# Two layers of a hybrid diffusion backbone on one core: the opening's loads and turns in another order, turned tiles repeated at the seams, and weight splits, gate blocks and one pair of loads moved

## The chip, the cores and the metric

The kernel runs on one core of a Trainium2 chip, as one launch, with nothing else on the chip. The time is the device time of one launch in microseconds. The engines of the core are named as in the profile: PE is TensorE (matmul; PEld its weight load), DVE is VectorE, ACT is ScalarE, POOL is GpSimd and SP is SyncE, which here issues all DMAs. Every engine runs its own instruction list in order and waits on semaphores that other engines raise.

## What is computed

The reference is one inference step of `DEPTH = 2` layers over 128 prompt tokens and 256 sample tokens of width 1024, all in float32. The two groups share the weights.

```python
def layer(x, mod, p, latent, ckv_ctx, krope_ctx, hf0, hb0):
    sh1, sc1, g1, sh2, sc2, g2 = jnp.split(mod, N_MOD, axis=-1)
    h = rms_norm(x, p["g_pre_mix"]) * (1.0 + sc1) + sh1
    y, ckv, krope, hf, hb = mixer(h, p, latent, ckv_ctx, krope_ctx, hf0, hb0)
    x = x + g1 * rms_norm(y, p["g_post_mix"])
    h = rms_norm(x, p["g_pre_ffn"]) * (1.0 + sc2) + sh2
    x = x + g2 * rms_norm(swiglu(h, p), p["g_post_ffn"])
    return x, ckv, krope, hf, hb
```

`mod` is `silu(c) @ w_mod + b_mod`, with six parts per layer. The mixer multiplies `h` by one wide `w_in` and takes from it the queries' and keys' latents, the input and gate of a bidirectional recurrence (a convolution over four tokens, sigmoid gates from block-diagonal weights, two scans over the tokens), and two merge gates. Attention of 8 heads and the recurrence are projected (`w_o_mla`, `w_o_lru`), merged by the gates and projected again (`w_out`). The feed-forward part is a SwiGLU with 2816 hidden channels.

## The kernel before

**Products.** Activations lie with channels on the partitions, in chunks of 128 channels by 384 tokens. Each weight block is a *job* of a few loads of 128x1024 elements. To keep float32 accuracy each operand is split in a high and a low part, and each product is three matmuls: high by high (line 669), high by low (676) and low by high (677). A job's eight chunks take four output banks each. ACT makes the high part of a load (`highs`, line 1180), DVE the low part (`lows`, line 1556). Both walk the same list of loads, and a call names how far the walk is to have come, so that moving a call moves a 128x1024 instruction to another place of that engine's list. There are 3 buffers for raw loads, 5 for each part, and 2 for weights of `w_mod`. SP waits for a raw buffer to be free (line 553) or for a `w_mod` buffer (line 560), and nothing behind the waiting issue goes out.

**Order.** The order of work on each engine is written out by hand. `plan_loads` sets the order of the loads. On TensorE the jobs run one after the other: `lx0`, `lx1` (the recurrence's input), `qk`, `kr` (latents), `gg0`, `gg1` (its gate), four merge jobs, the up-projections, `ol0` and `ol1` with attention woven in, `om0`, `om1`, `wo`, eleven `fi` jobs and `fo`. `gates_between` puts a gate block of the recurrence (four banks, lines 896 to 898) behind a given product of a job: a product is one of the 32 pairs of 676 and 677. Some jobs *host* products of the next modulation with `w_mod` in spare columns of their banks (`HOSTED`, line 708), after their first and third load.

**Recurrence on DVE and ACT.** Per chunk, ACT applies the gates and exponentials (`lru_gates`, `lru_coefficients`); DVE does `squared_roots`, `scans` (two directions, line 1804 to 1818), `gated` and `xc_low`, between the low parts of the weights.

**Seams.** Where a norm lies between two jobs (from `wo` to `fi0` in both layers, from `fo` to the next layer's `lx0`), the result stands with tokens on the partitions, in tiles 1, 2 (samples) and 0 (prompt), taken in that order. For each tile and half, ACT sums squares of the result (`y_square`), DVE scales it and adds it to `x` (`residual`), ACT sums squares of the new `x` and forms the inverse root (`x_square`: square, `sum_bias`, square, `root`), and writes it as a diagonal matrix `rstd`. TensorE multiplies `x` by the diagonal (line 629), which turns it to channels on the partitions and scales it at once (`turned`, `turn_first`). Then DVE and ACT make the activation's high and low part, chunk by chunk (`normalise`, `act_highs`).

**Opening.** SP loads the conditioning rows (`cache_c`), `ident`, `fold`, `x`, then 2 MB blocks of `w_mod` (`first_mod`) in two halves (`FIRST`), with the small parameter rows between. TensorE first transposes the conditioning rows, from which ACT makes `cs`; it turns the three tiles of `x`, multiplies the blocks by `cs` (`first_product`, line 838) and folds the sums (`first_fold`, line 848). The second half's products and folds stand inside job `lx0` (`opening_between`). The chunks 4 to 7 of `x` reuse the banks of the chunks 0 to 3, once ACT has moved those.

## Time and profile before

| what | value |
|---|---|
| median of 3 runs | 1329.72 us (1329.58 to 1330.15) |
| profiled execution | 1329.25 us, span 1327.5 us |
| TensorE busy | 1283.3 us, 97% of the span |
| DVE busy | 813.7 us, 61% |
| ACT busy | 661.8 us, 50% |
| granted TensorE clock, mean | 0.994 of full speed |
| DMA | 147 GB/s from HBM over the span |

The profiled execution is one launch of its own. Its span runs from the first to the last recorded instruction, and its time is what the launch reported. Busy time of TensorE is modelled: matmuls overlap, so an engine at 97% may still lose time at a lower clock. Granted clock 1.00 is 2.4 GHz and 0.50 is 1.2 GHz.

### The profile page before, as it was taken

Reading aid. Unit: us, or ns where it says so; the run is one execution under the profiler, and the core shown is the slowest. Engines: PE = TensorE matmul, PEld = TensorE weight load, DVE = VectorE, ACT = ScalarE, POOL = GpSimd, SP = SyncE. Lnnn points to the kernel's source line nnn. Section 1 sums busy time; section 2 is a strip of 40 time slices with the busy share of each in tenths; the row PEclk is TensorE's granted clock in tenths of the full one; section 3 lists DMA queues with packets and bytes.
Section 4 is the critical chain, followed back from the end, with each engine's and each line's share of the span. In section 5 each row is a group of like instructions: output and inputs, shape, how many; then the busy total and the mean of one; then the engine's idle time right before and its main releaser. Section 6 shows DMA issues by size and latency. Waiting matters only on the chain.

```text
span 1327.5 us, 20006 instructions
## 1 busy us (share of the span) xinstructions
PE 1283.3 (97%) x7691; PEld 1177.8 (89%) x7691; DVE 813.7 (61%) x1410; ACT 661.8 (50%) x1173; POOL 18.3 (1%) x38
## 2 busy tenths in 40 slices
PE   6999999999999999999999989999999999999998
PEld 4898999977879999998789989998788899999886
DVE  2687584763759877743367785747566785444424
ACT  4478873753454323342264989537444533333422
POOL 0000000200000000000000000002000000000000
PEclk9999999999999999999989999999999999999999
DMA  9535555323427766534325444553225374444431
GB/s 336 190 113 163 186 156 190 103 95 115 139 75 217 222 207 207 155 129 156 105 64 158 129 162 161 158 197 125 89 72 159 98 234 134 127 127 127 159 108 67
DMA packets 135058, 196.21 MB, mean 148 GB/s; under 512 B 9730, under 2 KB 68268, under 8 KB 134964
## 3 DMA queue, kind: packets, MB, share of 16 engines
q1 hardware_dynamic: 134964, 194.94, 45.9%
q8 instruction: 61, 1.00, 0.3%
q14 instruction: 33, 0.27, 0.1%
HBM read 193.03 MB, written 1.88 MB: 147 GB/s over the span
## 4 chain that ended last, share of the span: by engine, by line
PE 84%; DVE 5%; ACT 5%; DMA 3%; issue 2%; SPq 1%; DVEq 0%; ACTq 0%
PE bank L669 17%; PE bank L676 17%; PE bank L677 17%; PE bank L764 6%; PE bank L763 6%; PE bank L762 6%; DVE weight_low L1556 2%; PE bank L708 2%; DMA first_mod<-in_w_mod 2%; ACT weight_high L1180 1%; PE bank L1054 1%; PE bank L629 1%; PE bank L744 1%; PE bank L1078 1%; ACT sq L1188 1%
## 5 line engine op out<-in xcount | busy, mean ns | idle before, releaser
L676 PE MATMUL bank<-act_low,weight_high 128*128 128x384 f32 x1440 | 487.2, 338 | 4.6 <-DVE weight_low L1556 2.4
L677 PE MATMUL bank<-act_high,weight_low 128*128 128x384 f32 x1440 | 482.5, 335 | 0.0
L1556 DVE TENSOR_TENSOR weight_low<-raw,weight_high 128x1024 fp32r<-128x1024 f32 (+5 forms) x282 | 319.5, 1152 | 177.2 <-ACT weight_high L1180 176.7
L1180 ACT ACTIVATE weight_high<-raw 128x1024 fp32r<-128x1024 f32 (+5 forms) x282 | 273.4, 995 | 246.5 <-PE bank L764 77.1
L669 PE MATMUL bank<-act_high,weight_high 128*128 128x384 f32 x1440 | 316.5, 340 | 1.8 <-DVE t L1660 1.8
L676 PEld LDWEIGHTS bank<-act_low,weight_high 128*128 128x128 f32 x1440 | 271.2, 188 | 11.6 <-issue 4.9
L677 PEld LDWEIGHTS bank<-act_high,weight_low 128*128 128x128 f32 x1440 | 271.1, 188 | 0.0
L669 PEld LDWEIGHTS bank<-act_high,weight_high 128*128 128x128 f32 x1440 | 253.1, 189 | 8.4 <-issue 4.5
L762 PE MATMUL bank<-weight_high,hid_high 128*128 128x512 f32 x264 | 104.4, 395 | 0.0
L764 PE MATMUL bank<-weight_high,hid_low 128*128 128x512 f32 x264 | 102.8, 389 | 0.0
L763 PE MATMUL bank<-weight_low,hid_high 128*128 128x512 f32 x264 | 102.8, 389 | 0.0
L1518 ACT ACTIVATE sq<-bank 128x384 f32<-128x384 f32 x44 | 19.3, 490 | 149.7 <-PE bank L677 149.7
L2086 DVE TENSOR_TENSOR t<-bank,sq 128x384 f32<-128x384 f32 x44 | 24.5, 558 | 93.2 <-PE bank L677 90.0
L763 PEld LDWEIGHTS bank<-weight_low,hid_high 128*128 128x128 f32 x264 | 49.6, 188 | 11.2 <-issue 1.0
L762 PEld LDWEIGHTS bank<-weight_high,hid_high 128*128 128x128 f32 x264 | 49.6, 188 | 11.1 <-issue 1.0
L764 PEld LDWEIGHTS bank<-weight_high,hid_low 128*128 128x128 f32 x264 | 49.6, 188 | 10.3
L1472 ACT ACTIVATE sq<-bank 128x384 f32<-128x384 f32 (+1 forms) x48 | 20.2, 420 | 54.6 <-PE bank L1078 27.5
L629 PE MATMUL bank<-rstd,x 128*128 128x128 f32 x192 | 32.5, 321 | 15.1 <-ACT rstd L1226 13.3
L629 PEld LDWEIGHTS bank<-rstd,x 128*128 128x128 f32 x192 | 29.3, 226 | 20.1 <-issue 16.1
L2025 DVE TENSOR_REDUCE negmax<-bank 128x1 f32<-128x384 f32 (+1 forms) x48 | 22.1, 465 | 31.8 <-PE bank L1054 31.7
L762 PE MATMUL bank<-weight_high,act_high 128*128 128x512 f32 x96 | 39.0, 407 | 0.0
L1579 DVE SCALAR_TENSOR_TENSOR qkv<-mod_weight,cs,qkv 128x512 f32<-128x512 f32 x56 | 38.5, 746 | 0.0
(238 smaller groups left out, 1553.2 us busy)
## 6 DMA issues: line engine op xcount, KB each, us to landing
raw<-in_w_ffn_in SPq DMA_DIRECT2D x176, 256.0 KB, 3.7
mod_weight<-in_w_mod SPq DMA_DIRECT2D x80, 512.0 KB, 4.7
raw<-in_w_in SPq DMA_DIRECT2D x72, 512.0 KB, 4.5
raw<-in_w_ffn_out SPq DMA_DIRECT2D x44, 512.0 KB, 3.7
first_mod<-in_w_mod SPq DMA_DIRECT2D x4, 2048.0 KB, 15.1
raw<-in_w_o_lru SPq DMA_DIRECT2D x16, 512.0 KB, 3.7
raw<-in_w_out SPq DMA_DIRECT2D x16, 512.0 KB, 3.7
raw<-in_w_o_mla SPq DMA_DIRECT2D x8, 512.0 KB, 6.0
```

The costliest lines, as they stand in the source:

```text
L629: ins = nc.tensor.matmul(turn_bank(job, c)[:, P * a:P * a + P], x[:, a, P * c:P * c + P], rstd[:, P * a:P * a + P], start=True, stop=True)
L669: nc.tensor.matmul(bank(job, g)[:, 0:T], view[0][:, kk, cols], high[:, k, :], start=k == 0, stop=False)
L676: nc.tensor.matmul(o, view[0][:, kk, cols], low[:, k, :], start=False, stop=False)
L677: ins = nc.tensor.matmul(o, view[1][:, kk, cols], high[:, k, :], start=False, stop=k == total - 1)
L708: ins = nc.tensor.matmul(bank(job, b)[32 * q:32 * q + 32, T:512], cs[:, k, :], modw[MIDX[n] % MODR][:, 512 * kk + P * b:512 * kk + P * b + P],
L762: nc.tensor.matmul(o, high[:, k, toks], view[0][:, kk, :], start=k == 0, stop=False)
L763: nc.tensor.matmul(o, high[:, k, toks], view[1][:, kk, :], start=False, stop=False)
L764: ins = nc.tensor.matmul(o, low[:, k, toks], view[0][:, kk, :], start=False, stop=k == 2 * pairs - 1)
L1180: nc.scalar.activation(high, w, ACT.Copy).then_inc(*AC.step())
L1556: nc.vector.tensor_tensor(low, w, high.bitcast(F), ALU.subtract).then_inc(*VE.step())
L1579: nc.vector.scalar_tensor_tensor(out=total(r, g), in0=w, scalar=c, in1=total(r, g), op0=ALU.mult, op1=ALU.add).then_inc(*VE.step())
L2086: nc.vector.tensor_tensor(t[c % 2][:, :], bank(f"fi{j}", 2 + g)[:, 0:T], sq[c % 4][:, :], ALU.mult).then_inc(*VE.step("hid", c))
```

## The change

Eight edits are made together.

- SP issues `x_prompt`, `ident` and `x_sample` first, then the conditioning rows and `fold`.
- TensorE runs the first half's first product before it turns tile 2, and turns the chunks 4 to 7 together ahead of the second product. In `normalise` of layer 0, DVE makes the low part of a weight one chunk later.
- The third and fourth quarter of the `w_mod` block that `ol1` hosts are loaded behind `om0`'s first load instead of ahead of it.
- The four gate blocks of `qk` stand behind products 5, 11, 17 and 23 instead of 9, 13, 20 and 25.
- In `turn_first`, TensorE repeats the turns of the chunks 2 and 3 of the tiles 1 and 2 (four matmuls with the same operands into the same banks), ahead of the wait for tile 0.
- At a seam, ACT leaves out `sum_bias` of tile 0's new `x`. DVE computes the same number behind `residual`, once ACT's first square is done, and ACT waits for it before `root`.
- ACT makes the high parts of `gates1`'s first load and of `gg1`'s first load together, earlier; and those of `gg1`'s third load and `gates1`'s second load together, one gate earlier.
- DVE makes the low part of `gg0`'s third load ahead of `scans(0, 0)`, those of `gg1`'s first and `gates1`'s first load ahead of `scans(2, 2)`, `gg1`'s second ahead of `scans(3, 3)`, and `gates1`'s second ahead of `gated(5)`.

```diff
--- before.py
+++ after.py
@@ -100,8 +100,10 @@
                 loads.append(Load(("sum", r), 2, 512, False, [("rows", "w_mod", 2 * q, 2, r * 512, 512, 0)]))
-            if job in HOSTED and i in (0, 3):
+            if job in HOSTED and (i == 0 or i == 3 and job != "ol1"):
                 mod(HOSTED[job], (0, 1) if i < 3 else (2, 3))
+            if (job, i) == ("om0", 0):
+                mod(HOSTED["ol1"], (2, 3))
             if i in (0, 2) and gates_after is not None:
@@ -433,12 +435,12 @@
         def _(sp):
+            sp.dma_start(x[:, 0, :], A["x_prompt"].rearrange("b t d -> (b t) d")).then_inc(start_x[0], 16)
+            sp.dma_start(ident[:, :], A["ident"]).then_inc(start_load, 16)
+            sp.dma_start(x[:, 1:3, :], A["x_sample"].rearrange("b (a p) d -> p (b a) d", p=P)).then_inc(start_x[1], 16)
             sp.dma_start(cache_c[0:C, 0:P], A["c_ctx"].rearrange("(n p) -> n p", p=P)).then_inc(start_load, 16)
             sp.dma_start(cache_c[C:2 * C, 0:P], A["c"].rearrange("b (n p) -> (b n) p", p=P)).then_inc(start_load, 16)
-            sp.dma_start(ident[:, :], A["ident"]).then_inc(start_load, 16)
             sp.dma_start(fold[:, :], A["fold"]).then_inc(start_fold, 16)
-            sp.dma_start(x[:, 0, :], A["x_prompt"].rearrange("b t d -> (b t) d")).then_inc(start_x[0], 16)
-            sp.dma_start(x[:, 1:3, :], A["x_sample"].rearrange("b (a p) d -> p (b a) d", p=P)).then_inc(start_x[1], 16)
 
@@ -806,6 +808,10 @@
                             turned(atp, pre, job, c, (a,), f"turn{a}", layer=lp)
+                    for a in (1, 2):
+                        for c in (2, 3):
+                            nc.tensor.matmul(turn_bank(job, c)[:, P * a:P * a + P], x[:, a, P * c:P * c + P], rstd[:, P * a:P * a + P],
+                                             start=True, stop=True)
                     for c in range(4):
@@ -861,21 +867,19 @@
                     for a in range(3):
+                        if a == 2:
+                            first_product(0, 0)
                         pe.wait_ge(start_x[min(a, 1)], 16)
                             turned(at, "mix", "fo", c, (a,), "turned" if a == 2 else f"turned{a}", layer=0)
-                    first_product(0, 0)
-                    for c in (4, 5):
-                        pe.wait_ge(*at(AC, "moved", c - 4))
-                        turned(at, "mix", "fo", c, range(3), "turned", layer=0)
                     pe.wait_ge(*at(rows_full, "all"))
                     first_fold(0, 0)
+                    for c in range(4, C):
+                        pe.wait_ge(*at(AC, "moved", (c - 4, c - 2)[c > 5]))
+                        turned(at, "mix", "fo", c, range(3), "turned", layer=0)
                     first_product(0, 1)
-                    for c in (6, 7):
-                        pe.wait_ge(*at(AC, "moved", c - 2))
-                        turned(at, "mix", "fo", c, range(3), "turned", layer=0)
                     first_fold(0, 1)
@@ -959,7 +963,7 @@
 
-                split_job("qk", hh, hl, between=gates_between(0, (9, 13, 20, 25)))
+                split_job("qk", hh, hl, between=gates_between(0, (5, 11, 17, 23)))
                 split_job("kr", hh, hl, groups=[slice(0, P), slice(160 - P, 160)])
@@ -1217,10 +1221,14 @@
                         ac.wait_ge(*ready)
-                    square(x[:, a, 512 * h:512 * h + 512], 6 + 2 * a + h)
+                    by_vector = a == 0 and ready is not None
+                    square(x[:, a, 512 * h:512 * h + 512], 6 + 2 * a + h, *(("first_half", pre) if by_vector and h == 0 else ()), layer=lp)
                     if h == 0:
-                        sum_bias(6 + 2 * a, 15 + a)
+                        if not by_vector:
+                            sum_bias(6 + 2 * a, 15 + a)
                     else:
+                        if by_vector:
+                            ac.wait_ge(*in_layer(lp)(VE, "first_half", pre))
                         root(7 + 2 * a, 15 + a, 21 + a)
@@ -1378,12 +1386,12 @@
                 highs("gg0", 0)
-                lru_coefficients(0, {1: ("gg0", 1), 3: ("gg0", 2), 5: ("gg0", 3), 7: ("gg1", 0), 9: ("gates1", 0)})
+                lru_coefficients(0, {1: ("gg0", 1), 3: ("gg0", 2), 5: ("gg0", 3), 7: ("gates1", 0)})
                 for c in range(4):
                 highs("gg1", 1)
-                lru_gates(1, (("gg1", 2), ("gates1", 1), ("gg1", 3), ("m2a", 0)))
+                lru_gates(1, (("gates1", 1), ("gates1", 1), ("gg1", 3), ("m2a", 0)))
                 for c in range(4):
@@ -1689,7 +1697,7 @@
 
-                def residual(job, post):
+                def residual(job, post, pre, lp):
 
@@ -1713,6 +1721,10 @@
                         add(a, 1)
+                    if pre is not None:
+                        ve.wait_ge(*in_layer(lp)(AC, "first_half", pre))
+                        nc.vector.tensor_scalar(ss[:, 15:16], ss[:, 6:7], 1.0 / D, EPS, ALU.mult, ALU.add
+                                                ).then_inc(*VE.step("first_half", pre, layer=lp))
 
@@ -1745,7 +1757,7 @@
                         gain(scale1, 1, "g_pre_mix", ("scale1", half), chunks)
-                        normalise("mix", 0, "fo", "lx0", scale1, 0, ({1: 1}, {5: 3})[half], range(C)[chunks])
+                        normalise("mix", 0, "fo", "lx0", scale1, 0, ({2: 1}, {6: 3})[half], range(C)[chunks])
                 own()
@@ -1863,24 +1875,22 @@
                 squared_roots(1)
+                lows("gg0", 2)
                 scans(0, 0)
-                lows("gg0", 2)
                 squared_roots(2)
                 squared_roots(3)
-                lows("gg1", 0)
+                lows("gates1", 0)
                 scans(2, 2)
-                lows("gates1", 0)
+                lows("gg1", 1)
                 scans(3, 3)
-                lows("gg1", 1)
 
                 xc_low(6)
-                lows("gg1", 2)
+                lows("gates1", 1)
                 gated(5)
                 xc_low(7)
-                lows("gates1", 1)
                 gated(6)
@@ -2068,7 +2078,7 @@
                 lows("fi0", 0)
-                residual("wo", "mix")
+                residual("wo", "mix", "ffn", l)
                 normalise("ffn", l, "wo", "fi0", scale2, 3, {1: 1, 3: 2, 5: 3}, early=(0, 1))
@@ -2104,7 +2114,7 @@
                     lows("lx0", 0, layer=l + 1)
-                residual("fo", "ffn")
+                residual("fo", "ffn", *(("mix", l + 1) if l + 1 < DEPTH else (None, None)))
                 if l + 1 < DEPTH:
```

The list of TensorE at the very start, from its first transpose. `rstd,x` are the turns (x12: the chunks 0 to 3 of three tiles), `first_mod,cs` a first product, `mod_fold,ybuf` a fold. Before:

```order
L637 MATMUL bank<-ident,cache_c 128x16
L629 MATMUL bank<-rstd,x 128x128 x12
L838 MATMUL bank<-first_mod,cs 32x512 x8
L629 MATMUL bank<-rstd,x 128x128 x6
L872 MATMUL bank<-ident,rows_a 128x120
L873 MATMUL bank<-ident,rows_b 128x69
L848 MATMUL bank<-mod_fold,ybuf 128x2 x4
L838 MATMUL bank<-first_mod,cs 32x512 x8
L629 MATMUL bank<-rstd,x 128x128 x6
L848 MATMUL bank<-mod_fold,ybuf 128x2 x4
```

and in the changed kernel:

```order
L639 MATMUL bank<-ident,cache_c 128x16
L631 MATMUL bank<-rstd,x 128x128 x8
L844 MATMUL bank<-first_mod,cs 32x512 x8
L631 MATMUL bank<-rstd,x 128x128 x4
L876 MATMUL bank<-ident,rows_a 128x120
L877 MATMUL bank<-ident,rows_b 128x69
L854 MATMUL bank<-mod_fold,ybuf 128x2 x4
L631 MATMUL bank<-rstd,x 128x128 x12
L844 MATMUL bank<-first_mod,cs 32x512 x8
L854 MATMUL bank<-mod_fold,ybuf 128x2 x4
```

Four of the first twelve turns now follow the first product, and the twelve turns of the chunks 4 to 7 stand in one piece ahead of the second product and behind the first fold.

The list of DVE in the gate stretch of the first layer. `weight_low` is a weight's low part, `lru_tau<-t` a pair of `squared_roots`, and the rows from `lru_i<-lru_i` to `lru_h<-lru_h` one `scans`. Before:

```order
L1556 TENSOR_TENSOR weight_low<-raw,weight_high 128x1024
L1829 SCALAR_TENSOR_TENSOR lru_tau<-t,lru_tau 128x384 x2
L1804 TENSOR_TENSOR lru_i<-lru_i,lru_tau 128x384 x2
L1808 SCALAR_TENSOR_TENSOR lru_h<-lru_r,lru_i 128x128
L1808 SCALAR_TENSOR_TENSOR lru_h<-lru_r,par,lru_i 128x256
L1812 SCALAR_TENSOR_TENSOR lru_tau<-lru_r,lru_i 128x128
L1812 SCALAR_TENSOR_TENSOR lru_tau<-lru_r,par,lru_i 128x256
L1815 COPY hst<-lru_h 128x1
L1816 COPY hst<-lru_tau 128x1
L1818 TENSOR_TENSOR lru_h<-lru_h,lru_tau 128x384
L1556 TENSOR_TENSOR weight_low<-raw,weight_high 128x1024
L1829 SCALAR_TENSOR_TENSOR lru_tau<-t,lru_tau 128x384 x2
```

and in the changed kernel:

```order
L1564 TENSOR_TENSOR weight_low<-raw,weight_high 128x1024
L1841 SCALAR_TENSOR_TENSOR lru_tau<-t,lru_tau 128x384 x2
L1564 TENSOR_TENSOR weight_low<-raw,weight_high 128x1024
L1816 TENSOR_TENSOR lru_i<-lru_i,lru_tau 128x384 x2
L1820 SCALAR_TENSOR_TENSOR lru_h<-lru_r,lru_i 128x128
L1820 SCALAR_TENSOR_TENSOR lru_h<-lru_r,par,lru_i 128x256
L1824 SCALAR_TENSOR_TENSOR lru_tau<-lru_r,lru_i 128x128
L1824 SCALAR_TENSOR_TENSOR lru_tau<-lru_r,par,lru_i 128x256
L1827 COPY hst<-lru_h 128x1
L1828 COPY hst<-lru_tau 128x1
L1830 TENSOR_TENSOR lru_h<-lru_h,lru_tau 128x384
L1841 SCALAR_TENSOR_TENSOR lru_tau<-t,lru_tau 128x384 x2
```

The second `weight_low`, `gg0`'s third load, stood behind the scans and stands ahead of them.

The list of SP around `ol1` (`w_o_lru`) and `om0` (`w_o_mla`). Before:

```order
L567 DMA raw<-in_w_o_lru 128x2x512 x5
L567 DMA mod_weight<-in_w_mod 128x2x512 x2
L567 DMA raw<-in_w_o_lru 128x2x512 x3
L567 DMA mod_weight<-in_w_mod 128x2x512 x2
L567 DMA raw<-in_w_o_mla 128x2x512 x4
L567 DMA raw<-in_w_out 128x2x512 x4
```

and in the changed kernel:

```order
L569 DMA raw<-in_w_o_lru 128x2x512 x5
L569 DMA mod_weight<-in_w_mod 128x2x512 x2
L569 DMA raw<-in_w_o_lru 128x2x512 x3
L569 DMA raw<-in_w_o_mla 128x2x512
L569 DMA mod_weight<-in_w_mod 128x2x512 x2
L569 DMA raw<-in_w_o_mla 128x2x512 x3
```

The first of the `w_o_mla` loads now stands ahead of the two `mod_weight` loads.

## Rows read from the trace of the kernel before

**Rows 1.** Head of the page.

```profile
span 1327.5 us, 20006 instructions
```

**Rows 2.** Timeline of the opening: start, length (us), engine, line, instruction, [idle before, releaser].

```profile
2.40 0.43 SPq L440 DMA_DIRECT2D x<-in_x_prompt  x1
...
3.42 0.26 PE L637 MATMUL bank<-ident,cache_c 16*128 16x16 f32 x1 [3.42 <-DMA ident<-in_ident]
...
3.92 1.28 ACT L1276 ACT_TABLE_LOAD   x1
...
5.99 0.63 ACT L1188 ACTIVATE sq<-x 128x512 f32<-128x512 f32 x1 [0.78 <-DMA x<-in_x_prompt]
...
8.93 0.63 ACT L1188 ACTIVATE sq<-x 128x512 f32<-128x512 f32 x1 [0.29 <-DMA x<-in_x_sample]
...
11.73 2.05 PE L629 MATMUL bank<-rstd,x 128*128 128x128 f32 x8 [0.90 <-ACT rstd L1226]
...
16.26 3.64 PE L838 MATMUL bank<-first_mod,cs 128*32 128x512 f32 x16
...
22.59 1.92 PE L838 MATMUL bank<-first_mod,cs 128*32 128x512 f32 x16
```

**Rows 3.** DMA issues of 0 to 60 us: size, median us from issue to landing.

```profile
rot<-in_rot SPq DMA_DIRECT2D x1, 64.0 KB, 7.8
```

**Rows 4.** TensorE's timeline of the first block, rows with idle before them.

```profile
32.59 0.45 PE L676 MATMUL bank<-act_low,weight_high 128*128 128x384 f32 x1 [0.93 <-DVE act_low L1670]
...
36.83 1.92 PE L838 MATMUL bank<-first_mod,cs 128*32 128x512 f32 x16 [0.71 <-DMA first_mod<-in_w_mod]
...
49.02 0.45 PE L676 MATMUL bank<-act_low,weight_high 128*128 128x384 f32 x1 [1.28 <-DVE act_low L1670]
```

**Rows 5.** Timelines of ACT, DVE and TensorE in the first layer's gate stretch.

```profile
98.96 0.47 ACT L1374 ACTIVATE sq<-bank 128x384 f32<-128x384 f32 x1
...
111.82 1.05 ACT L1180 ACTIVATE weight_high<-raw 128x1024 fp32r<-128x1024 f32 x1
...
116.27 1.22 DVE L1556 TENSOR_TENSOR weight_low<-raw,weight_high 128x1024 fp32r<-128x1024 f32 x1
...
124.25 1.22 DVE L1556 TENSOR_TENSOR weight_low<-raw,weight_high 128x1024 fp32r<-128x1024 f32 x1
...
117.55 0.45 PE L676 MATMUL bank<-act_low,weight_high 128*128 128x384 f32 x1 [1.18 <-DVE weight_low L1556]
...
130.50 0.44 PE L896 MATMUL bank<-xc_high,weight_high 128*128 128x384 f32 x1 [1.59 <-DVE weight_low L1556]
...
142.35 0.34 PE L677 MATMUL bank<-act_high,weight_low 128*128 128x384 f32 x1
143.68 0.44 PE L896 MATMUL bank<-xc_high,weight_high 128*128 128x384 f32 x1 [0.98 <-DVE weight_low L1556]
```

**Rows 6.** SP's waits of 280 to 330 us, then timelines of ACT and TensorE.

```profile
SPq L560 <- PE bank L708: 24.2, 1, 24.2
...
309.78 1.06 ACT L1180 ACTIVATE weight_high<-raw 128x1024 fp32r<-128x1024 f32 x1 [3.62 <-DMA raw<-in_w_o_mla]
...
311.45 0.49 PE L1054 MATMUL bank<-keys,q_last 96*128 96x128 f32 x2 [1.48 <-ACT sq L1486]
312.97 0.52 PE L1063 MATMUL bank<-ident,sq 128*128 128x128 f32 x3 [1.03 <-DVE sq L2013]
```

**Rows 7.** Timeline of the first seam.

```profile
387.04 1.41 DVE L1707 SCALAR_TENSOR_TENSOR x<-ybuf,sums,x 128x512 f32<-128x512 f32 x2
...
388.77 0.61 ACT L1188 ACTIVATE sq<-x 128x512 f32<-128x512 f32 x1
...
390.61 1.90 PE L629 MATMUL bank<-rstd,x 128*128 128x128 f32 x14 [2.28 <-ACT rstd L1226]
```

**Rows 8.** Windows: stretch, length, busy time of each engine (instructions), granted clock, DMA share, GB/s.

```profile
683.30:689.30 6.00, 5.99 (x23) 6.00 (x24) 4.78 (x10) 3.28 (x6) 0.00 (x0) 0.50 0.21 51
1040.90:1044.30 3.40, 3.40 (x17) 3.40 (x16) 3.02 (x6) 2.16 (x4) 0.00 (x0) 0.50 0.02 5
```

## The prediction

> **What bounds the kernel now.** I began with the head of the page: the profiled execution spans 1327.5 us [rows 1], and reported 1329.25 us, so 1.75 us lie around the span. I then went through TensorE's own timeline, keeping only rows with an idle time in brackets. The reader is to see that they are few and short: eight in the opening and first block, three in each layer's gate stretch, six in each layer's attention, two at each of three seams. Between them TensorE issues without a hole. So a microsecond counts only if it removes a TensorE wait, removes TensorE work, or moves TensorE from the half clock to the full one. What DVE and ACT gain elsewhere is worth nothing. A bracket understates its delay a little, since the modelled ends overlap: the product at 142.35 is printed with 0.33 us, but its kind start every 0.17 us, so the next slot was 142.52 and the start at 143.68 is 1.16 late where the bracket says 0.98 [rows 5]. I add 0.17 per removed wait.
>
> **The change, part by part.**
>
> *Opening.* `start_load` needs ident and both `cache_c` loads. Before, these headed the queue and TensorE ran its transpose at 3.42; ACT then loaded a table (3.92 to 5.20) and squared tile 0 at 5.99, held by x [rows 2]. Now x_prompt and x_sample (1.5 MB) stand ahead of the two 4 KB loads. x_sample landed at 8.93, where ACT's second tile waited for it. All of x moves up by what stood ahead of x_prompt's issue at 2.40, four issues like its own of 0.43 [rows 2], less 0.2 for ident: 7.4. Do the small loads wait for it? Of small loads behind big ones the trace has one fair witness: the constant `rot`, 64 KB, issued behind 4 MB of `first_mod`, took 7.8 us to land [rows 3]. I take them as waiting: transpose at 7.5, and 1.8 us later (3.42 to 5.20) the first square at 9.3, 3.3 us late. Tiles 1 and 2 become 3.0 late, as tile 1 was held for x_sample. Tile 1's turn ended at 13.78 [rows 2], now 16.8. The Trainium skill ("DMA: Bandwidth & Descriptors", Queues, rings and completion order) says each of the 16 engines consumes a ring in order, and that a small copy uses only some rings; the 7.8 us agrees. If the small loads passed x instead, the opening would gain 2.2 us, worked out under the rivals.
>
> From there TensorE's old chain was 16.26 (first product) to 24.51 (end of the second) = 8.25 us [rows 2]. The new one also holds tile 2's turn (2.05) and chunks 6 and 7 (1.6 for 12 passes at full clock): 11.9. It ends at 28.7 to 28.9, 4.3 late. The fold behind it no longer waits for those chunks (0.3), so the first block starts 4.0 late. In it the 0.93 wait goes (its cause, the weight's low part, now stands one chunk later), the two second-half products follow without the 0.71 wait for `first_mod` [rows 4], and the reordered low part removes the 1.28 wait. Sum: 4.0 - 0.93 - 0.71 - 1.28 - 2 x 0.17 = +0.7, and 0.1 to 0.2 in step gaps: **+0.5**. Bounds: +3 if the reordering removes nothing, -2.2 as above.
>
> *Gate stretch, each layer.* Three waits, 1.18, 1.59 and 0.98 [rows 5]. The first is for the low part of gg0's third load, which DVE made at 116.27, behind `scans(0, 0)`, though ACT had the high part ready at 111.82 + 1.05 = 112.87. Now it stands ahead of them: 112.87 + 1.22 = 114.1, and TensorE wants it at 116.4. The second wait is for gates1's first load, behind `scans(2,2)`; now it is ahead of these. The third is for gates1's second load, whose high part ACT now makes one gate earlier. DVE's rows carry no idle from there to 124.25 + 1.22 = 125.47, the end of gg1's first low part [rows 5], and this is what becomes late next: TensorE, 1.35 us ahead, wants it at 124.6. The gate blocks moved in `qk` pay here. Gate block 3 issues 2.7 us earlier, so ACT is free when `qk`'s first bank is done (about 98.0, not 98.96 [rows 5]); ACT and DVE behind it run 0.95 earlier, and the low part is ready at 124.95 allowing for a 0.45 wait of DVE that overlaps this. Left: 0.4. The gate blocks themselves cost nothing: the earliest, at product 5 (74.8), needs DVE's copies of the second lx block, done 1.3 us before. So 3.75 + 3 x 0.17 - 0.4 = 3.9 per layer, **-7.7**. Bounds: 0 (DVE merely moves the waits) and -8.6.
>
> *ol1's hosted loads.* SP stood 24.2 us at line 560 on TensorE's products, and om0's first load was queued behind it. ACT waited 3.62 us for that load, was on it until 310.8, and TensorE waited 1.48 and 1.03 [rows 6]. Now the load is issued ahead of the blocking wait, about 20 us earlier, and ACT copies it at 306.2, 3.6 us before. The hosted loads still follow at 303; om0's second load, which they now precede, lands near 309 and ACT wants it at 319. 2.51 + 0.34 - 0.3 (what such a copy costs at its neighbours) = 2.5 per layer, the second having the same pair: **-5.0**. Bounds: -3 and -5.6.
>
> *Seams (three).* ACT squares tile 0's second half at 388.77, behind the bias step that is now taken out; DVE had that half of x ready at 387.04 + 1.41 = 388.45 [rows 7]. With the semaphore and the read of the accumulator ahead of it the square can start at 388.55, 0.22 earlier. DVE's new 128x1 instruction, some 0.17 us like the other tiny ones, is hidden in 0.5 us of ACT's square; it delays the early chunks of the samples by 0.3, and they have 0.5. 3 x 0.22 = **-0.7**. The four extra products (eight passes, 1.16 us like the row before the wait) fit in the wait of 2.28, now 2.06 [rows 7]; 0.9 of idle remains. Their direct cost is nothing as long as the wait is over 1.16.
>
> *Clock.* Granted clock is 0.50, the 1.2 GHz level, in three stretches: 6.0 us after the second seam, 3.4 after the third, and another 3.4 after the first layer's om0 wait, TensorE busy throughout [rows 8]. Before each it had waited 2.3 to 2.9 us in about 4. With the extra products no more than 0.6 + 0.9 is left around a seam, and the om0 wait is gone. All three stretches then run at 2.4 GHz. Upper bound half of 12.8 = 6.4; DVE and ACT pace a little of it, so I take 0.9 of that, **-5.8**. Lower bound 0.
>
> Sum: +0.5 - 7.7 - 5.0 - 0.7 - 5.8 = -18.7. From 1329.25 that is 1310.6; the median of the runs lies 0.5 above the profiled one, hence 1311.0.
>
> **Rivals.**
> 1. *The clock still falls at a seam.* For it: the first seam had the same 2.28 wait and turned its next 14 passes in 1.90 us, at full clock [rows 7], so the fall hangs on more than the wait's length. Against: idle is halved. Price 1.7 to 4.7: 1314. The Trainium skill ("TensorE: Matmul & The Clock Gate", What's actually happening) says half rate is the resting state and activity releases it, watched on a count that is not aligned to the program. By that rule the same idle may or may not cost: the 1314 of this rival.
> 2. *The small loads are not held.* Then tile 2 is ready as before; the chain starts at 13.8 and ends at 26.1, 1.6 late, and `first_mod`'s last part, 1.7 earlier with the whole stream, no longer holds it: opening -2.2, 1308.4.
> 3. *The gate waits move instead of going.* DVE is full from 112 to 135, and I left only 0.1 us of slack at gg0's last low part. If ACT's 0.95 doesn't come, 0.9 per layer returns, and if gates1 still waits for the bank that ACT empties, 1.5 more: 1313 to 1316.
> 4. *Slower than before.* The late start of ACT delays TensorE's first full clock. The first product took 3.64 us, the second, 6 us later, 1.92 [rows 2], so the opening begins at half clock and rises in between. Each further microsecond at half costs 0.5; it decides from about 37 us longer, deep into lx1, where nothing in the trace keeps TensorE idle. Then 1330 or more.
> 5. *No change*: everything removed returns as other waits. Only if DVE's work, not its order, bounded; its idle rows elsewhere speak against.
>
> **How the numbers follow.** My forecast 0.50 (own range 1308.5 to 1313.5), rival 1 0.17, rival 2 0.12, rival 3 0.14, rival 4 0.04, rival 5 0.03. The range that leaves out under 2 in 10 is 1306.5 to 1317. About 0.2% is what a measurement of this kernel can tell from no change. Faster 0.93 (forecast and rivals 1 to 3), within 0.03, slower 0.04.
>
> **What would show it.** Opening: ACT's first square near 9.3 and first block near 32.6; at 6.4 and 29.7 rival 2 holds. Gate stretch: no TensorE bracket near 116, 129 and 142, at most one of 0.4 on gg1's first low part. om0: SP issues it before the hosted loads, and ACT has no wait on it. Seams: eight more passes, a wait near 0.9, clock 1.00. I am wrong if the small loads hold the opening for more than 3 us, if the brackets reappear one load later, or if a 0.50 stretch remains.

## The result and the profile after

The changed kernel took 1310.5 us in the median of 4 runs (1308.53 to 1312.94), the kernel before 1329.93 (1329.58 to 1332.02) beside it. The ratio is 0.9852, 95% interval 0.9832 to 0.9871. The profiled execution has a span of 1305.7 us, 21.8 less than [rows 1], and reported 1308.53 us, the lowest of the four.

Head of the page of the changed kernel:

```profile
span 1305.7 us, 20057 instructions
```

TensorE's timeline of the changed kernel, the rows with idle before them (start, length, engine, line, instruction, [idle, releaser]). From 123.68 on they repeat in the second layer and at the second and third seam to 0.05 us.

```profile
8.06 0.25 PE L639 MATMUL bank<-ident,cache_c 16*128 16x16 f32 x1 [8.06 <-DMA cache_c<-in_c]
12.65 2.05 PE L631 MATMUL bank<-rstd,x 128*128 128x128 f32 x8 [4.34 <-ACT rstd L1234]
...
16.85 1.92 PE L844 MATMUL bank<-first_mod,cs 128*32 128x512 f32 x16
...
26.59 1.02 PE L854 MATMUL bank<-mod_fold,ybuf 128*128 128x2 f32 x8 [0.91 <-DVE ybuf L1734]
29.43 1.05 PE L671 MATMUL bank<-act_high,weight_high 128*128 128x384 f32 x4 [1.81 <-DVE t L1668]
...
123.68 0.44 PE L678 MATMUL bank<-act_low,weight_high 128*128 128x384 f32 x1 [0.31 <-DVE weight_low L1564]
...
286.93 0.52 PE L1067 MATMUL bank<-ident,sq 128*128 128x128 f32 x3 [0.67 <-DVE sq L2023]
...
376.96 1.16 PE L631 MATMUL bank<-rstd,x 128*128 128x128 f32 x8 [0.59 <-DVE ybuf L1708]
...
380.19 1.90 PE L631 MATMUL bank<-rstd,x 128*128 128x128 f32 x14 [1.17 <-ACT rstd L1234]
```

The waits of 0.93, 0.71 and 1.28 us [rows 4], of 1.18, 1.59 and 0.98 [rows 5] and of 1.48 and 1.03 [rows 6] are gone; 0.31 stands on `gg1`'s first low part. At the seam 1.17 is left of 2.28 [rows 7]. The 0.91 ahead of the fold (26.59) is new: no turns stand between the second product and the fold any more. Windows of the changed kernel (stretch, length, busy time of PE, PEld, DVE, ACT, POOL, granted clock, DMA share, GB/s) over a stretch at the start of `lx0`, over the place behind the first layer's `om0` wait and over the two places that [rows 8] shows at 0.50:

```profile
30.10:33.50 3.40, 3.40 (x13) 3.40 (x12) 3.29 (x7) 1.56 (x3) 0.00 (x0) 0.50 1.05 387
304.10:307.50 3.40, 3.40 (x24) 2.88 (x24) 0.85 (x4) 0.84 (x3) 0.00 (x0) 1.00 0.57 204
672.60:678.60 6.00, 5.91 (x41) 5.92 (x42) 4.92 (x10) 3.58 (x6) 0.00 (x0) 1.00 0.25 63
1020.00:1023.40 3.40, 3.32 (x23) 3.33 (x24) 2.44 (x5) 2.77 (x4) 0.00 (x0) 1.00 0.00 0
```

Of the kernel before, [rows 8] shows two of its three half-clock stretches. This is the third, with TensorE's wait of `om0` in the second layer, behind which no stretch stood (window, then timeline of before):

```profile
313.90:317.20 3.30, 3.30 (x10) 2.74 (x9) 0.00 (x0) 0.47 (x3) 0.00 (x0) 0.50 0.36 137
```

```profile
962.82 0.49 PE L1054 MATMUL bank<-keys,q_last 96*128 96x128 f32 x2 [1.25 <-ACT sq L1486]
```

Three old half-clock stretches are gone and a new one of 3.4 us stands at the start of `lx0`. (At the very start the column says 1.00 although eight passes take 2.05 us there and 1.16 later; only their durations show the half clock.)

Where the 21.8 us come from is read by laying the two lists of TensorE over each other and noting the same instruction's start in both. The offset changes only where a wait or a stretch went:

| up to | start before | start after | offset | this stage | predicted |
|---|---|---|---|---|---|
| second block of lx0, last wait | 49.31 | 47.99 | -1.3 | -1.3 | +0.5 |
| end of gate stretch, layer 1 | 143.96 | 138.37 | -5.6 | -4.3 | -3.9 |
| om0 waits, layer 1 | 312.97 | 304.37 | -8.6 | -3.0 | -2.5 |
| clock behind them | 317.32 | 307.10 | -10.2 | -1.6 | -1.5 |
| second seam, wait | 683.32 | 672.69 | -10.6 | -0.4 | -0.5 |
| clock behind it | 689.32 | 675.99 | -13.3 | -2.7 | -2.7 |
| gate stretch, layer 2 | 795.74 | 778.15 | -17.6 | -4.3 | -3.9 |
| om0 waits, layer 2 | 964.34 | 944.26 | -20.1 | -2.5 | -2.5 |
| third seam, wait and clock | 1044.29 | 1022.53 | -21.8 | -1.7 | -1.8 |

(The prediction's clock term of 5.8 is shared out here by the stretches' lengths.) Everything but the first row came as forecast, to 0.5 us. So the opening was what there was to test, and with it the changed kernel's own spread of 4.4 us, where the kernel before has 2.4.

### The profile page after: what moved, and what is told of

It is laid out like the page before. It is cut to its first block, busy times and chain, and to the rows that moved or that the text cites. A ratio compares the mean times of both kernels' runs of the same rounds, so it can differ in the third digit from the quotient of the medians.

```text
span 1305.7 us, 20057 instructions
## 1 busy us (share of the span) xinstructions
PE 1275.4 (98%) x7715; PEld 1175.4 (90%) x7715; DVE 813.2 (62%) x1413; ACT 661.1 (51%) x1170; POOL 18.2 (1%) x38
## 4 chain that ended last, share of the span: by engine, by line
PE 88%; ACT 5%; DVE 4%; issue 2%; DMA 0%; SPq 0%; DVEq 0%; ACTq 0%
PE bank L671 18%; PE bank L678 18%; PE bank L679 18%; PE bank L766 5%; PE bank L765 5%; PE bank L764 5%; ACT sq L1192 2%; PE bank L710 2%; DVE weight_low L1564 1%; PE bank L631 1%; PE bank L1058 1%; PE bank L1082 1%; PE bank L746 1%; ACT weight_high L1184 1%; PE bank L1067 1%
## 5 line engine op out<-in xcount | busy, mean ns | idle before, releaser
L631 PE MATMUL bank<-rstd,x 128*128 128x128 f32 x192 | 28.6, 293 | 10.1 <-ACT rstd L1234 8.4
L1587 DVE SCALAR_TENSOR_TENSOR ybuf<-mod_weight,cs,ybuf 128x512 f32<-128x512 f32 x56 | 38.4, 745 | 0.0
```

What stands on the lines that cost most here:

```text
L631: ins = nc.tensor.matmul(turn_bank(job, c)[:, P * a:P * a + P], x[:, a, P * c:P * c + P], rstd[:, P * a:P * a + P], start=True, stop=True)
L1587: nc.vector.scalar_tensor_tensor(out=total(r, g), in0=w, scalar=c, in1=total(r, g), op0=ALU.mult, op1=ALU.add).then_inc(*VE.step())
```

## The experiments

Each was timed beside the kernel before on the same chip; kernels with the same median of before were timed together. `small_first` turned out steadier and faster than the changed kernel, so later edits were made to it.

| kernel | median (range) us | before beside it | difference |
|---|---|---|---|
| after_again | 1311.58 (1309.23 to 1312.54) | 1329.57 | -18.0 |
| small_first | 1307.67 (1307.16 to 1308.17) | 1329.57 | -21.9 |
| turns_old | 1310.10 (1309.5 to 1311.62) | 1329.57 | -19.5 |
| lx_low_old | 1312.97 (1311.48 to 1315.05) | 1329.57 | -16.6 |
| no_repeat_sf | 1311.18 (1310.95 to 1311.84) | 1328.97 | -17.8 |
| before_repeat | 1325.62 (1324.7 to 1328.25) | 1328.97 | -3.4 |
| mod_first_sf | 1315.23 (1314.88 to 1316.78) | 1328.97 | -13.7 |
| splits_old_sf | 1314.03 (1313.76 to 1314.32) | 1328.97 | -14.9 |
| blocks_old_sf | 1309.78 (1309.46 to 1310.28) | 1329.39 | -19.6 |
| small_turns_old | 1307.04 (1306.88 to 1307.96) | 1329.39 | -22.4 |
| gg1_low_first | 1308.52 (1308.36 to 1309.5) | 1329.39 | -20.9 |
| opening_filled | 1305.28 (1304.69 to 1306.29) | 1329.66 | -24.4 |

**after_again**: no edit.

> The changed kernel once more, unaltered, to see how far its own executions differ. Its first four gave 1308.5 to 1312.9 us where the kernel before gave 1329.6 to 1332.0, and the one trace has TensorE at the half clock from 29.4 to 33.3 us, which costs 1.9. Theory: the opening's clock is a matter of chance from one execution to the next; then the half-clock stretches of the opening stand elsewhere in this trace, and TensorE's first block of lx0 still starts within 2 us of 29.4. Rival: the clock follows from the order of the work, and the stretches stand where they stood, to 0.1 us. Both expect 1310.5, and no half clock at the seams.

TensorE's opening in this second trace of the changed kernel:

```profile
9.61 0.26 PE L639 MATMUL bank<-ident,cache_c 16*128 16x16 f32 x1 [9.61 <-DMA cache_c<-in_c]
...
18.72 2.62 PE L844 MATMUL bank<-first_mod,cs 128*32 128x512 f32 x16
...
32.00 1.62 PE L671 MATMUL bank<-act_high,weight_high 128*128 128x384 f32 x4 [1.81 <-DVE t L1668]
```

Its half-clock stretch at `lx0` (window):

```profile
30.43:37.26 6.83, 5.26 (x17) 5.29 (x17) 5.93 (x14) 3.54 (x6) 0.00 (x0) 0.50 1.06 374
```

The transpose, which waits for the 4 KB load behind `x`, came 1.55 us later, and the first product ran partly at half clock (2.62 where the first trace has 1.92): `lx0` starts 2.57 us later in the same program. The half-clock stretch at its start is there again, at another place and longer (TensorE is idle in it until 32.0). The stretch of the first trace is 3.4 us long, so it cost about 1.7 and not the 1.9 of the expectation, which took the whole window from 29.4 to 33.3 for it. Every later wait is the same to 0.05 us. So the expected "within 2 us" was too narrow and the rival's fixed clock is out; the opening differs by some 3 us from one execution to the next.

**small_first**: the small loads ahead of `x`.

```diff
-            sp.dma_start(x[:, 0, :], A["x_prompt"].rearrange("b t d -> (b t) d")).then_inc(start_x[0], 16)
-            sp.dma_start(ident[:, :], A["ident"]).then_inc(start_load, 16)
-            sp.dma_start(x[:, 1:3, :], A["x_sample"].rearrange("b (a p) d -> p (b a) d", p=P)).then_inc(start_x[1], 16)
             sp.dma_start(cache_c[0:C, 0:P], A["c_ctx"].rearrange("(n p) -> n p", p=P)).then_inc(start_load, 16)
             sp.dma_start(cache_c[C:2 * C, 0:P], A["c"].rearrange("b (n p) -> (b n) p", p=P)).then_inc(start_load, 16)
+            sp.dma_start(ident[:, :], A["ident"]).then_inc(start_load, 16)
+            sp.dma_start(x[:, 0, :], A["x_prompt"].rearrange("b t d -> (b t) d")).then_inc(start_x[0], 16)
+            sp.dma_start(x[:, 1:3, :], A["x_sample"].rearrange("b (a p) d -> p (b a) d", p=P)).then_inc(start_x[1], 16)
```

> The changed kernel with the opening's loads in the order conditioning rows, ident, x_prompt, x_sample, fold. Theory (the small loads were held behind x): TensorE's transpose comes at 3 instead of 8.1 us and ACT's first square at 5.5 instead of 9.85, bound by x_prompt. TensorE's first product is then bound by first_mod, which lands near 14.5, and starts 2.3 earlier; the first block of lx0 starts 1 to 2 earlier, near 28; of that no more than 0.8 stays, since the last part of first_mod lands near 36.3 and the last product of the opening starts at 37.2 now. 0.3 to 0.8 us less than the changed kernel, near 1310. Rival: if the clock rises later than at 16 us because the work is spread thinner, the gain is eaten: 0 to 1.7 more than that.

TensorE's timeline of it, and below that ACT's first square:

```profile
3.56 0.26 PE L639 MATMUL bank<-ident,cache_c 16*128 16x16 f32 x1 [3.56 <-DMA ident<-in_ident]
...
14.03 3.64 PE L844 MATMUL bank<-first_mod,cs 128*32 128x512 f32 x16 [0.81 <-DMA first_mod<-in_w_mod]
...
29.17 1.21 PE L671 MATMUL bank<-act_high,weight_high 128*128 128x384 f32 x4 [1.81 <-DVE t L1668]
```

```profile
5.64 0.63 ACT L1192 ACTIVATE sq<-x 128x512 f32<-128x512 f32 x1 [0.31 <-DMA x<-in_x_prompt]
```

The mechanism is as expected, and TensorE is now held by `first_mod`. The size is not: 3.9 us less than the changed kernel on the same chip (2.8 less than its first four runs, on another), where 0.3 to 0.8 was expected. I had sized it by the one trace in which the transpose came at 8.06, the earliest of four. This trace by itself spans 0.4 us more than that one and 3.1 less than the one of `after_again`. With the edit the spread shrinks from 3.3 to 1.0 us.

**turns_old**: TensorE's opening of before in the changed kernel.

```diff
                     for a in range(3):
-                        if a == 2:
-                            first_product(0, 0)
...
+                    first_product(0, 0)
+                    for c in (4, 5):
...
                     first_fold(0, 0)
-                    for c in range(4, C):
...
                     first_product(0, 1)
+                    for c in (6, 7):
...
                     first_fold(0, 1)
```

> The changed kernel with TensorE's opening in the order of before (three tiles, first product, chunks 4 and 5, fold, second product, chunks 6 and 7); loads and low parts stay as changed. Theory: the order of the turns is worth little, since tile 2's diagonal is ready at 17.6 and the old chain of 8.25 us, without 1.7 at the half clock, ends its second product near 25.3 against 25.7 now, with the turns of chunks 6 and 7 behind it: first block at 29.4 as now, 0 to 0.5 us more. Rival: the new order is what kept the opening from being 4 us late; then the first block starts at 31 to 33 and the kernel takes 1.5 to 3.5 more.

1310.10 against 1311.58, ranges overlapping. These runs show no gain from the new order of the turns.

**lx_low_old**: `({1: 1}, {5: 3})` again in `normalise` of layer 0.

> The changed kernel with DVE's low parts of lx0's weights behind chunks 1 and 5 again (2 and 6 in the change). Theory: the waits of 0.93 and 1.28 us for an act_low in the first and second block of lx0 come back, 0.1 to 0.2 more each for the restart: 2.4 us more than the changed kernel, near 1313. Rival: the first of them is taken up by the wait for the last part of first_mod, which TensorE reaches later; then 1.4 more.

```profile
36.15 0.44 PE L678 MATMUL bank<-act_low,weight_high 128*128 128x384 f32 x1 [0.90 <-DVE act_low L1678]
...
51.70 0.45 PE L678 MATMUL bank<-act_low,weight_high 128*128 128x384 f32 x1 [1.31 <-DVE act_low L1678]
```

Both waits of [rows 4] are back in this timeline of TensorE. The median is 1.4 us more, not 2.4, and the ranges overlap (1311.48 to 1315.05 against 1309.23 to 1312.54). The trace has none of the half-clock stretch at `lx0`, which its neighbours have; that hides some of the cost in this trace, and the medians cannot part the two.

**no_repeat_sf**: `small_first` without the four repeated turns.

```diff
-                    for a in (1, 2):
-                        for c in (2, 3):
-                            nc.tensor.matmul(turn_bank(job, c)[:, P * a:P * a + P], x[:, a, P * c:P * c + P], rstd[:, P * a:P * a + P],
-                                             start=True, stop=True)
```

> small_first (the changed kernel with the conditioning rows and ident loaded ahead of x, 1307.7 us) without the four repeated turns at each seam. TensorE's wait for tile 0's diagonal goes from 1.17 back to about 2.07 us at three seams, 0.2 under the 2.28 of the kernel before. Theory (idle around the seam lets the clock fall): half-clock stretches come back at one to three seams, as two of the three seams had them before, at 2.7 and 1.5 us; 1.5 to 4.5 us more than small_first, 1309 to 1312. Rival: the falls of before came with the longer wait, and 2.07 is under it: 0 to 0.3 more, all at 2.4 GHz.

The turns behind the wait at its three seams (timeline), and the windows from there on:

```profile
379.63 2.61 PE L631 MATMUL bank<-rstd,x 128*128 128x128 f32 x14 [2.07 <-ACT rstd L1230]
...
673.68 2.98 PE L631 MATMUL bank<-rstd,x 128*128 128x128 f32 x14 [2.07 <-ACT rstd L1230]
...
1022.31 3.32 PE L631 MATMUL bank<-rstd,x 128*128 128x128 f32 x14 [2.06 <-ACT rstd L1230]
```

```profile
379.60:383.60 4.00, 3.97 (x19) 3.97 (x20) 3.09 (x6) 2.72 (x4) 0.00 (x0) 0.62 0.00 0
673.60:677.90 4.30, 4.22 (x20) 4.25 (x21) 3.40 (x7) 2.79 (x5) 0.00 (x0) 0.60 0.01 4
1022.30:1025.70 3.40, 3.39 (x15) 3.40 (x16) 2.41 (x4) 2.71 (x4) 0.00 (x0) 0.51 0.02 5
```

14 passes that take 1.90 at 2.4 GHz now take 2.6 to 3.3, at all three seams, the first among them, which had been spared in the kernel before. 3.5 us more than `small_first`, 4.1 by the kernels before beside them. The clock theory holds; the rival, that a wait of 2.07 might be short enough, is out.

**before_repeat**: those four lines added to the kernel before, and nothing else.

> The kernel before with the four repeated turns at each seam and nothing else changed. Theory: the wait for tile 0's diagonal is 1.1 to 1.3 instead of 2.28, the half-clock stretches of 6.0 and 3.4 us at the second and third seam go, 4.2 us are won, and the 3.4 us after the first layer's om0 wait stay: near 1325.5. Rival: the seams fall for what lies ahead of them and not for this wait; then nothing changes, 1329.6.

Timeline of the last seam:

```profile
1037.07 1.90 PE L629 MATMUL bank<-rstd,x 128*128 128x128 f32 x14 [1.39 <-ACT rstd L1230]
```

Window behind the second layer's `om0` wait:

```profile
959.30:962.60 3.30, 3.00 (x11) 3.03 (x12) 0.71 (x4) 0.97 (x5) 0.00 (x0) 0.50 0.53 159
```

3.35 us less, ratio 0.9971 (0.996 to 0.9982), with 1.90 at all three seams. More matmuls, less time. It is under the 4.2 expected. The stretch that was to stay behind the first layer's `om0` wait is not in this trace and one stands behind the second layer's, with the same waits of 1.36 and 1.03 in both layers; and `lx0` has one too (27.4 to 30.9), as in the changed kernel. The wait is 1.39 here and 1.17 in the changed kernel: the 0.22 between them is what the bias step on DVE gives, as forecast.

**mod_first_sf**: `small_first` with the hosted loads ahead of `om0`'s first.

```diff
-            if job in HOSTED and (i == 0 or i == 3 and job != "ol1"):
+            if job in HOSTED and i in (0, 3):
                 mod(HOSTED[job], (0, 1) if i < 3 else (2, 3))
-            if (job, i) == ("om0", 0):
-                mod(HOSTED["ol1"], (2, 3))
```

> small_first with ol1's hosted loads of the third and fourth quarter ahead of om0's first load again. Theory: ACT waits 3.6 us for om0's first load in each layer, TensorE has 1.48 and 1.03 of wait behind it, 2.7 to 3.0 per layer: 5.7 us more, and 1.6 more if the clock falls behind the first layer's wait as it did before: 1313.4 to 1315. Rival: with everything earlier by the same amount the load is in time anyway, or its wait is taken up elsewhere in the layer: under 2 more.

ACT's timeline, then the window behind the second layer's wait:

```profile
304.29 1.06 ACT L1182 ACTIVATE weight_high<-raw 128x1024 fp32r<-128x1024 f32 x1 [3.66 <-DMA raw<-in_w_o_mla]
```

```profile
952.00:956.00 4.00, 4.00 (x14) 3.09 (x12) 0.00 (x0) 0.84 (x3) 0.00 (x0) 0.57 0.36 128
```

The wait of 3.62 [rows 6] is back, and TensorE's two behind it, in both layers. 7.6 us more than `small_first`, above the 5.7 to 7.3 expected. In its trace the clock fell in the second layer too: TensorE is 4.9 us behind `small_first` after the first layer's `om0` and 8.5 after the second's.

**splits_old_sf**: `small_first` with the splits of before (DVE's part; ACT's walk likewise).

```diff
-                lows("gg0", 2)
                 scans(0, 0)
+                lows("gg0", 2)
...
-                lows("gates1", 0)
+                lows("gg1", 0)
                 scans(2, 2)
-                lows("gg1", 1)
+                lows("gates1", 0)
                 scans(3, 3)
+                lows("gg1", 1)
...
-                lows("gates1", 1)
+                lows("gg1", 2)
                 gated(5)
                 xc_low(7)
+                lows("gates1", 1)
```

> small_first with the weight splits of gg0, gg1 and gates1 where they were before on ACT and DVE; the gate blocks of qk stay at 5, 11, 17 and 23. Theory: the three waits of 1.18, 1.59 and 0.98 us come back but the one of 0.31 goes, each a little shorter since ACT and DVE run 0.9 earlier behind qk: 2.5 to 4.2 per layer, 5 to 8.4 in all, 1313 to 1316. Rival: the moved gate blocks alone remove most of the waits, and this costs under 3 us in all.

**blocks_old_sf**: `small_first` with `gates_between(0, (9, 13, 20, 25))`.

> small_first with the four gate blocks of qk behind products 9, 13, 20 and 25 again, splits as changed. Theory (the moved blocks give ACT, and DVE behind it, 0.95 us at the end of qk): the wait for gg1's first low part grows from 0.30 to about 1.2 us in each layer, 1.5 to 2.2 us more in all, near 1309.5. Rival: DVE has idle of 2.8 us ahead of its second low part there, the lateness is taken up by it, and nothing changes.

TensorE's timeline of `splits_old_sf`, and then of `blocks_old_sf`:

```profile
115.27 0.44 PE L678 MATMUL bank<-act_low,weight_high 128*128 128x384 f32 x1 [0.17 <-DVE weight_low L1564]
...
128.23 0.45 PE L900 MATMUL bank<-xc_high,weight_high 128*128 128x384 f32 x1 [1.57 <-DVE weight_low L1564]
...
141.41 0.44 PE L900 MATMUL bank<-xc_high,weight_high 128*128 128x384 f32 x1 [0.99 <-DVE weight_low L1564]
```

```profile
124.47 0.45 PE L678 MATMUL bank<-act_low,weight_high 128*128 128x384 f32 x1 [1.30 <-DVE weight_low L1564]
```

The two edits work apart. The splits are worth 6.4 us (3.3 per layer in the traces): with the old ones, two of the three waits of [rows 5] return in full and the first as 0.17, since the moved gate blocks had already taken 1.0 of its 1.18. The blocks are worth 2.1 us: without them the 0.30 on `gg1`'s first low part is 1.30, in both layers. ACT's first latent stands at 97.43 without the move and at 96.34 with it. Together they give the 8.5 us of the table.

**gg1_low_first**: can the last 0.30 go as well?

```diff
+                lows("gg1", 0)
                 squared_roots(3)
                 lows("gates1", 0)
```

> small_first with DVE's low part of gg1's first load ahead of squared_roots(3) instead of behind. Theory: it is ready 0.9 us earlier, the wait of 0.30 us goes in each layer with its restart of 0.1, 0.8 us less in all, near 1306.9. Rival: the square roots come 1.2 us later, ACT with them, and the banks that ACT empties for gg1's gate blocks come late: 0.5 to 2 more per layer.

TensorE's timeline, then ACT's:

```profile
127.00 0.41 PE L900 MATMUL bank<-xc_high,weight_high 128*128 128x384 f32 x1 [0.95 <-DVE lru_h L1820]
```

```profile
123.56 0.94 ACT L1365 ACTIVATE lru_tau<-lru_tau,epsc 128x768 f32<-128x768 f32 x1 [1.77 <-DVE lru_tau L1841]
124.54 0.85 ACT L1367 ACTIVATE lru_tau<-lru_tau 128x768 f32<-128x768 f32 x1
125.29 1.61 ACT L1392 ACTIVATE ybuf<-bank 128x384 f32<-128x384 f32 x4
```

0.9 us more than `small_first`. The wait is gone and 0.95 stands at the next gate block. The row names DVE's scan, but a gate block also waits for its banks to be free, and what ends at 126.9 is ACT's emptying of four banks (125.29 + 1.61), 1.2 us late behind the square roots. The rival was right.

**small_turns_old**: `small_first` with TensorE's opening of before (the diff of `turns_old`).

> small_first with TensorE's opening in the order of before. Theory: with x early, the second first_product is held by the load, which lands near 21.5; in the order of before it starts at 21.9 instead of 23.5, and the first block of lx0 at about 28.0 instead of 29.2; the last part of first_mod, near 36.3, takes back most of it: 0 to 1.2 us less than small_first. Rival: the order of the change was right with x early too, since tile 2 comes ahead of the first product: 0.5 to 1 more.

**opening_filled**: `small_turns_old`, with the fold between the last two turned chunks and chunk 7 turned twice.

```diff
-                    for c in (6, 7):
-                        pe.wait_ge(*at(AC, "moved", c - 2))
-                        turned(at, "mix", "fo", c, range(3), "turned", layer=0)
+                    pe.wait_ge(*at(AC, "moved", 4))
+                    turned(at, "mix", "fo", 6, range(3), "turned", layer=0)
                     first_fold(0, 1)
+                    pe.wait_ge(*at(AC, "moved", 5))
+                    for a in range(3):
+                        nc.tensor.matmul(turn_bank("fo", 7)[:, P * a:P * a + P], x[:, a, P * 7:P * 7 + P], rstd[:, P * a:P * a + P],
+                                         start=True, stop=True)
+                    turned(at, "mix", "fo", 7, range(3), "turned", layer=0)
```

> small_turns_old (small loads first, TensorE's opening in the order of before, 1307.0 us) with the second fold between the turns of chunks 6 and 7, and chunk 7 turned twice. Theory: the fold starts 0.4 us earlier, TensorE is busy in 1.6 of the 1.8 us of idle ahead of lx0, and the half-clock stretch of about 3.5 us at the start of lx0 goes: 0.4 and 1.7 us; the last part of first_mod, near 36.3, gives back up to 1: 0.6 to 2 less, 1305 to 1306.4. Rival: the stretch at lx0 does not hang on this idle (it is the same 1.81 us in the kernel before, whose trace has no such stretch); then 0 to 0.4 less.

Timelines of TensorE, `small_turns_old` first, then `opening_filled`; last the window of the latter from its first block on:

```profile
21.41 1.92 PE L844 MATMUL bank<-first_mod,cs 128*32 128x512 f32 x16 [0.50 <-DMA first_mod<-in_w_mod]
...
27.47 1.58 PE L671 MATMUL bank<-act_high,weight_high 128*128 128x384 f32 x4 [1.81 <-DVE t L1670]
```

```profile
24.88 0.91 PE L887 MATMUL bank<-rstd,x 128*128 128x128 f32 x6
25.62 0.83 PE L631 MATMUL bank<-rstd,x 128*128 128x128 f32 x6
26.82 0.93 PE L671 MATMUL bank<-act_high,weight_high 128*128 128x384 f32 x4 [0.36 <-DVE t L1674]
...
34.68 1.92 PE L844 MATMUL bank<-first_mod,cs 128*32 128x512 f32 x16 [1.60 <-DMA first_mod<-in_w_mod]
```

```profile
26.80:33.00 6.20, 6.18 (x40) 4.52 (x40) 4.44 (x9) 2.35 (x4) 0.00 (x0) 1.00 1.05 387
```

The old order starts `lx0` 1.7 us earlier than `small_first` when `x` comes early; 0.6 less in the median, ranges overlapping. The last edit brings 1.8 us more: `lx0` starts 0.65 earlier and runs at 2.4 GHz, and a wait of 1.60 for the last part of `first_mod` takes part of it back. How much is the earlier fold and how much the repeated turns was not parted. That the filled idle keeps the clock up rests on this trace and on the mean clocks of its five runs (0.998 to 1.000, against 0.996 to 0.999 for `small_turns_old`): two traces with the idle left open had no stretch at `lx0` either. 1305.28 us is the fastest version, ratio 0.9815 (0.9799 to 0.9831), 5.2 us under the changed kernel's 1310.5.

## Why the prediction was right, point by point

- **Gate stretch** (predicted -7.7): -8.5, with the next wait on `gg1`'s first low part, 0.31, where 0.4 was forecast. The size is a little under: each removed bracket was worth 0.27 more than it says (1.18 moved the offset from -1.32 to -2.77, that is 1.45), and I had taken 0.17. That the moved gate blocks pay 0.95 per layer was right (1.0, `blocks_old_sf`).
- **om0's first load** (-5.0): -5.5. SP, wait, ACT and TensorE moved as forecast; `mod_first_sf` brings them all back. I took the second layer's pair to be the same as the first's, but it was 1.25 and 1.03: -3.0 and -2.5, where I had -2.5 twice.
- **Seams** (-0.7): -0.6 in three steps of 0.2. The wait left is 1.17, not 0.9, since the eight repeated passes filled 0.9 of it (2.07 without them) and not 1.16; their direct cost is nothing, as forecast.
- **Clock** (-5.8): -5.8 in the trace. For the seams this is shown from both sides by `no_repeat_sf` and `before_repeat`. The 1.6 behind `om0` is one execution's draw: such a pair of waits (2.3 to 2.6 us of idle in all) was followed by a half-clock stretch in the first layer only in the kernel before, in the second only in `before_repeat`, and in both in `mod_first_sf`. Over its executions the kernel before reported mean clocks from 0.988 (1333.77 us) to 0.995 (1328.71 us). Rival 1, that the clock still falls at a seam, is out: 12 traces with the repeats have 36 seams, all with 1.90. Without them 5 of 6 fell. The Trainium skill ("TensorE: Matmul & The Clock Gate", What's actually happening) says that the count is not aligned to the program; the one seam of six that was spared, in the kernel before, agrees.
- **Opening** (+0.5): the mis-sized term. In the first trace it measured -1.3, in the second +2.1: `lx0` starts at 29.43 and 32.00 where I had 32.6. From there to the end of the second block's last wait the kernel before took 20.7 us, the changed one 18.6 and 19.4, so 2.1 and 1.3 were won where the removed waits were put at 3.3.

  That the small loads are held behind `x` was right: the transpose came at 8.06, 9.61, 9.86 and 9.99 in the four traces with `x` ahead (7.5 forecast) and at 3.40 to 4.03 with them ahead, and it costs 3.9 us (`small_first`). Rival 2 is out (its chain, by its own terms, ends at 13.8 + 11.9 = 25.7 and not at 26.1, and its -2.2 goes with 25.7). The time of the first block could not tell the two apart: 29.43 is the sign that was set for rival 2, and came with the loads held.

  Two things were not in the sum: the first product runs at full clock in one execution and partly at half in another (1.92 or 2.62 where I had 3.64), and TensorE falls to half at the start of `lx0`, which the trace of before did not show. Two of the prediction's own signs of being wrong have thus come: the small loads cost more than 3 us, and a stretch at 0.50 remains.

  In the second execution the terms are +2.1 - 8.5 - 5.5 - 0.6 - 5.8 = -18.3, as its span says (1309.2 against 1327.5): the opening is 1.6 over the forecast, the gate stretch and om0 1.3 under it, and so the sum of -18.7 was met more closely than its terms. The first execution misses it by 3.1. That the median lies 0.5 from the 1311.0 forecast is in this part luck.
- **Rival 3** did not come, but had the right places: without the moved blocks 1.0 per layer returns, where it had 0.9. Rivals 4 and 5 are out.

What stays open: what places the rise of the clock in the opening and its fall at `lx0`; whether `turns_old` and the changed kernel differ at all (1.5 us in the median, within their ranges); and how much of `lx_low_old` is its two waits and how much the clock.

## What to carry to other kernels

Read one trace's start-up as one draw: its loads and its clock moved this kernel by 3 us while every wait behind it repeated to 0.05 us, so compare two traces, or medians, before sizing anything there. A load that gates the first instruction belongs ahead of the bulk even when it is 4 KB. And where TensorE must wait 2 us, repeating a harmless product in the wait can be worth more than shortening the wait: here 0.2 us less of it left the clock falling at three of three seams, and the repeats at none.

## What the runs showed of the hardware

- Two 4 KB loads behind 1.6 MB of others, the last issued at 2.6 us: the transpose that waits for them ran 5.5 us later in the best of four traces and 7.4 in the worst. Ahead of the bulk it ran at 3.4 to 4.0 us, in ten traces, those of the kernel before among them.
- A wait of 2.07 to 2.28 us at a seam, some 1 us of turns behind one of 0.59, was followed by a half-clock stretch, with up to 6.0 us of work in it, at 5 of 6 seams; one of 1.17 to 1.39 at none of 36. Two waits of 2.3 to 2.6 us in all at `om0` were followed by one in 4 of 6 cases. Around 1.81 us of idle ahead of `lx0` the clock fell in 11 of 13 traces, around 0.36 not in the one.
- The granted clock's column reads 1.00 at the start of every trace while eight passes take 2.05 us there and 1.16 later.
